# A gated delta rule: two products of the scan made as one, the last transposed update left out, and the inverse's first triangle made one round earlier

## The chip, the cores and the metric

One core of a Trainium2 chip runs the whole kernel in one launch. The metric is the device time in microseconds (us) of that launch; of several runs, the median.

## What is computed

Two transformer blocks over 1024 tokens of width 1024, all in float32. The change touches one branch of the first block, the gated delta rule: 4 heads, keys and values of width 128, chunks of 64 tokens.

```python
kk = jnp.einsum('bhnid,bhnjd->bhnij', k, k)
m = jnp.where(strict, beta[..., :, None] * kk * decay, 0.0)
rhs = jnp.concatenate([beta[..., None] * v, beta[..., None] * k * jnp.exp(gc)[..., None]], axis=-1)
sol = lax.linalg.triangular_solve(eye + m, rhs, left_side=True, lower=True, unit_diagonal=True)
u, w = sol[..., :dv], sol[..., dv:]
...
def step(state, inp):
    qk_c, qd_c, kd_c, u_c, w_c, ge_c = inp
    v_new = u_c - jnp.einsum('bhck,bhkv->bhcv', w_c, state)
    o = (jnp.einsum('bhck,bhkv->bhcv', qd_c, state)
         + jnp.einsum('bhij,bhjv->bhiv', qk_c, v_new))
    state = state * ge_c[..., None, None] + jnp.einsum('bhck,bhcv->bhkv', kd_c, v_new)
    return state, o
```

So a chunk multiplies two matrices with the same state: w (64 by 128) and the decayed q (64 by 128).

## The kernel before, in words

The kernel is a row of phases with a barrier of all engines between them; SBUF and PSUM tiles are placed anew in each. The phase "delta" holds the change. Five stages share it, and each stage is a generator per engine that emits a piece of its instructions and yields. `run_stages` goes through one written-out list of stage numbers, the plan, and lets each engine's generators emit in that order. An engine runs its own instructions strictly in the order emitted; engines meet only through semaphores (`ev.wait` before, `ev.done` behind an instruction).

`delta_plan` (L1508) makes the plan from rounds: 3 opening rounds and then 10 periods of 14 rounds (s = 0 to 13). In each round come in this order

- DeltaFront (L949): in period t it prepares the tile of 128 tokens (two chunks) number t: turns q, k and v, norms, the decay matrix, `mt` (the masked product m, transposed; round 10), `qk_t` (round 11).
- DeltaBack (L1190): one period later it inverts eye + m for the tile, by 5 levels of block doubling. Round 0: the first triangle on VectorE, `bt0` and `upper0` (L1227, L1229: 128 by 512 each), four transposes of it on TensorE (L1268) and ScalarE's copy to `lower`. Then for each level an odd round with `bx` (L1277) and an even round with the two updates (L1284 for `lower`, L1285 for its transpose `upper`) and VectorE's two subtractions (L1233, L1234). Round 11: u (L1291); round 12: w (L1296), whose copy to SBUF is L1238.
- DeltaScan (L1301): one period later again it runs the recurrence over the tile's two chunks. In rounds 1 and 7 (`FIRST`) w by state (L1377) and q by state (L1382); in rounds 3 and 9 (`SECOND`) the growth of the state (L1390) and qk by v_new (L1394).
- TokenProjection (L1400): a projection of all tokens, 10 groups of 256 columns; one step of it is 12 matmuls in fp32r (L1500 to L1502); 162 steps are spread evenly over the rounds, mostly one each, sometimes two. Every fourth step ends with a copy on VectorE (L1486) and every fourth with one on ScalarE (L1476); two steps in sixteen split the next weights (ScalarE L1453, VectorE L1458).

GpSimd makes, among others, `vb` (L1114, round 12), `wr` (L1118, round 13) and the masked `bt` of each level (L1248; levels 1 and 2 in rounds 0 and 1).

A float32 product of one head is two instructions for TensorE, so the four heads show as x8; a transpose is one, so x4; an fp32r product is one.

The order of the rounds is what the change works on:

```python
        if t < TT:
            plan.append(0)
        if 1 <= t <= TT:
            plan.append(1)
        if t >= 2:
            plan.append(2)
        ...
        plan += [3] * (want - given)
```

Of the kernel before, what the change touches and what calls it, by code (L numbers as in the profile page):

```python
# [808 lines left out]
class Delta:  # L809
# [4 lines left out]
    def __init__(self, ph, nc, early, qkv, out, c):  # L814
        self.nc, self.early, self.c, self.qkv, self.out = nc, early, c, qkv, out
        H = self.H
        self.ba = ph.sb("ba", [P, TT, 2 * H])
        self.a_row, self.dt_row, self.mask, self.exp_a = early.a_row, early.dt_row, early.mask, ph.sb("exp_a", [P, H])
        self.x, self.clip, self.expx, self.softplus, self.g, self.rest = (
            ph.sb(n, [P, TT, H]) for n in ("x", "clip", "expx", "softplus", "g", "rest"))  # L820
        self.by_tile = ph.sb("by_tile", [P, TT, 4, H])
        self.beta, self.g_sum, self.exp_gc, self.exp_rest = (self.by_tile[:, :, i, :] for i in range(4))
        self.chunk_decay = ph.sb("chunk_decay", [P, 2, TT, H])
        self.xt, self.tok, self.t_sb = ph.sb("xt", [P, 3 * H, P]), ph.sb("tok", [P, 3, H, P]), ph.sb("t_sb", [P, 3, H, P])
        self.norm = ph.sb("norm", [P, 3, 2 * H])
        self.half = ph.sb("half", [P, 2 * H])
        (self.kn, self.qn, self.kb, self.vb, self.wr, self.qd, self.gb, self.decay, self.mt, self.upper, self.lower, self.bx,
         self.u, self.w_t, self.faded) = (
            ph.sb(n, [P, H, P]) for n in ("kn", "qn", "kb", "vb", "wr", "qd", "gb", "decay", "mt", "upper", "lower", "bx",
                                          "u", "w_t", "faded"))  # L830
        two = lambda n: [ph.sb(f"{n}{i}", [P, H, P]) for i in range(2)]
        self.bt, self.q_t, self.qk_t, self.k_end, self.state, self.v_new, self.o_sb = (
            two(n) for n in ("bt", "q_t", "qk_t", "k_end", "state", "v_new", "o"))
        self.front = [ph.ps(f"front{i}", [P, H, P]) for i in range(2)]
        self.back = [ph.ps(f"back{i}", [P, H, P]) for i in range(2)]
        self.ws, self.o = ph.ps("ws", [P, H, P]), ph.ps("o_acc", [P, H, P])
        self.xt_in, self.stored = ph.sem("xt_in"), ph.sem2("stored")
        self.pre = Events(ph, "pre", ["turned", "kept", "half", "exp_a", "beta", "x", "clip",
                                      "expx", "log", "softplus", "g", "sums", "gc", "rest", "exps"])
        self.ev = Events(ph, "tile", [  # L840
            "q_turned", "k_turned", "v_turned", "gc_rows", "kn_turned", "kb_turned", "qn_turned", "qd_turned", "kk", "qk_dot",
            "gb", "tok_q", "tok_k", "tok_v", "squares", "decay", "t_k", "t_kb", "t_q", "q_kept",
            "sums", "gap", "clamp", "kn", "kb", "qn", "masked", "mt", "qk",
            "means", "inverse", "k_end", "qd", "vb", "wr",
            "bt0", "upper0", "lower0_t", "lower0", "bt", "bx", "bx_kept", "update", "lower", "upper", "u_dot", "u", "w_dot", "w",
            "ws", "v_new", "faded", "grow", "state", "o_done", "o_out"])
# [4 lines left out]
    def over_heads(self, a):  # L851
        return a.unsqueeze(1).to_broadcast([P, self.H, P])


# [94 lines left out]
class DeltaFront:  # L949
# [18 lines left out]
    def scalar(self, act):  # L968
# [17 lines left out]
        for j in range(TT):  # L986
            for s in range(d.STEPS):
# [31 lines left out]
                elif s == 9:  # L1019
                    ev.wait(act, "qd_turned", j + 1)  # L1020
                    ev.wait(act, "o_done", 2 * (j - 1))
                    ev.done(nc.scalar.activation(d.q_t[j % 2][:], d.front[1][:], ACT.Copy), "q_kept")
                yield

    def vector(self, dve):
        d, ev, pre, nc, H = self.d, self.d.ev, self.d.pre, self.d.nc, self.d.H
        sums = lambda b: d.o[:, b, 0:TT * H].rearrange("p (m h) -> p m h", h=H)
        pre.wait(dve, "turned", 1)
        pre.done(nc.vector.tensor_copy(d.ba[:], d.ws[:, 0, 0:2 * TT * H].rearrange("p (m n) -> p m n", n=2 * H)), "kept")
        pre.wait(dve, "kept", 1)  # L1030
# [17 lines left out]
        for j in range(TT):  # L1048
            for s in range(d.STEPS):
# [28 lines left out]
                elif s == 11:  # L1078
                    ev.wait(dve, "qk_dot", j + 1)
                    ev.wait(dve, "o_done", 2 * (j - 1))  # L1080
                    ev.done(nc.vector.tensor_tensor(d.qk_t[j % 2][:], d.front[1][:], d.decay[:], ALU.mult), "qk")
                yield

# [37 lines left out]
    def tensor(self, pe):  # L1121
# [3 lines left out]
        for m in range(TT):  # L1125
            last = nc.tensor.transpose(d.ws[:, 0, m * 2 * H:(m + 1) * 2 * H], d.early.ba_t[:, m * P:(m + 1) * P],
                                       ident[0:2 * H, 0:2 * H])
# [62 lines left out]
class DeltaBack:  # L1190
# [28 lines left out]
    def vector(self, dve):  # L1219
        d, ev, nc, L = self.d, self.d.ev, self.d.nc, self.d.LEVELS  # L1220
        for j in range(TT):
            for s in range(d.STEPS):
                if s == 0:
                    ev.wait(dve, "mt", j + 1)
                    ev.wait(dve, "w_dot", j)
                    ev.wait(dve, "u_dot", j)
                    ev.done(nc.vector.tensor_tensor(d.upper[:], d.mt[:], d.over_heads(d.mask[:, 0, :]), ALU.mult), "bt0")  # L1227
                    ev.wait(dve, "bt0", j + 1)
                    ev.done(nc.vector.tensor_tensor(d.upper[:], d.over_heads(d.c["ident"][:]), d.upper[:], ALU.subtract), "upper0")  # L1229
# [28 lines left out]
    def tensor(self, pe):  # L1258
        d, ev, nc, H, L = self.d, self.d.ev, self.d.nc, self.d.H, self.d.LEVELS
        for j in range(TT):  # L1260
            for s in range(d.STEPS):
# [17 lines left out]
                elif s <= 2 * L and s % 2 == 0:  # L1279
# [21 lines left out]
class DeltaScan:  # L1301
# [8 lines left out]
    def chunk(self, i):  # L1310
        return i // 2, slice((i % 2) * CHUNK, (i % 2 + 1) * CHUNK), i % 2

    def sync(self, sp):
        d, ev = self.d, self.d.ev
        for j in range(TT):
            for s in range(d.STEPS):
                if s in (5, 11):
                    i = 2 * j + (s == 11)
                    _, rows, p = self.chunk(i)
                    ev.wait(sp, "o_out", i + 1)  # L1320
                    sp.dma_start(d.out[i * CHUNK:(i + 1) * CHUNK, :].rearrange("t (h d) -> t h d", d=P), d.o_sb[p][rows]
                                 ).then_inc(d.stored[p], 16)
# [7 lines left out]
    def scalar(self, act):  # L1330
        d, ev, nc = self.d, self.d.ev, self.d.nc
        for j in range(TT):
            for s in range(d.STEPS):
                if s in self.SECOND:
# [3 lines left out]
                    if i >= 2:  # L1338
                        act.wait_ge(d.stored[p], 16 * (i // 2))
                    ev.done(nc.scalar.activation(d.o_sb[p][rows], d.o[rows], ACT.Copy), "o_out")  # L1340
                yield

    def vector(self, dve):
        d, ev, nc, H = self.d, self.d.ev, self.d.nc, self.d.H
        ev.done(nc.vector.memset(d.state[0][:], 0.0), "state")
        for j in range(TT):
            for s in range(d.STEPS):
                if s in self.FIRST:
# [4 lines left out]
                    ev.wait(dve, "o_done", i - 1)  # L1353
                    ev.done(nc.vector.tensor_tensor(d.v_new[p][rows], d.u[rows], d.ws[rows], ALU.subtract), "v_new")
                    ev.wait(dve, "state", i + 1)
                    ev.done(nc.vector.tensor_tensor(d.faded[:], d.state[p][:], d.per_head(d.chunk_decay[:, i % 2, m, :]), ALU.mult),
                            "faded")
                elif s in self.SECOND:
# [4 lines left out]
                    ev.wait(dve, "o_done", i)  # L1363
                    ev.done(nc.vector.tensor_tensor(d.state[1 - p][:], d.faded[:], d.ws[:], ALU.add), "state")
                yield

    def tensor(self, pe):
        d, ev, nc, H = self.d, self.d.ev, self.d.nc, self.d.H
        for j in range(TT):
            for s in range(d.STEPS):  # L1370
                if s in self.FIRST:
# [3 lines left out]
                    ev.wait(pe, "w", j + 1)  # L1375
                    for h in range(H):
                        last = nc.tensor.matmul(d.ws[rows, h, :], d.w_t[:, h, rows], d.state[p][:, h, :], start=True, stop=True)  # L1377
                    ev.done(last, "ws")
                    ev.wait(pe, "q_kept", j + 1)
                    ev.wait(pe, "o_out", i)  # L1380
                    for h in range(H):
                        nc.tensor.matmul(d.o[rows, h, :], d.q_t[j % 2][:, h, rows], d.state[p][:, h, :], start=(h == 0), stop=False,  # L1382
                                         skip_group_check=True)
                elif s in self.SECOND:
# [4 lines left out]
                    for h in range(H):  # L1389
                        last = nc.tensor.matmul(d.ws[:, h, :], d.k_end[j % 2][rows, h, :], d.v_new[p][rows, h, :], start=True, stop=True)  # L1390
# [3841 lines left out]
```

## Time and profile before

| | us |
|---|---|
| median of 3 runs | 2673.11 |
| lowest, highest | 2672.35, 2676.2 |
| the profiled execution's own time | 2669.34 |
| its span, first to last instruction | 2667.6 |
| TensorE busy in the span | 2545.4 (95%) |
| VectorE, ScalarE, GpSimd busy | 1455.6 (55%), 998.5 (37%), 350.5 (13%) |
| mean granted TensorE clock | 0.983 of full speed |

The engines are PE (TensorE; PEld its weight loads), DVE (VectorE), ACT (ScalarE), POOL (GpSimd). Matmuls are pipelined: the duration shown of one is longer than the distance to the next, so the distance from start to start is what one costs. "Idle before" is time in which the engine had nothing under way, and the arrow names what ended it. A clock of 1.00 is 2.4 GHz, 0.50 is 1.2 GHz.

### The profile page before, as it was taken

To read this page: it belongs to the slowest core of one execution; us is meant where nothing else is said; L and a number is where in the kernel's file an instruction comes from. 1 tells how busy PE (TensorE), PEld (TensorE's weight loads), DVE (VectorE), ACT (ScalarE), POOL (GpSimd) and SP (SyncE) were. 2 spreads that over 40 slices of the span, in tenths; PEclk is the share of its full clock that TensorE was granted. 3 is DMA by queue.
4 is the path that set the end of the run, shared out by engine and by line. 5 is a ranking of instruction groups with operands and counts; after the bars stand their busy time and mean duration, and the time that the engine had idled before them with its cause. 6 is when DMAs were issued, how large, how long until landed. Compare 5 with 4: busy or idle time off the path is not lost. (4 is left out here: it accounts for less than half of the span.)

```text
span 2667.6 us, 37142 instructions
## 1 busy us (share of the span) xinstructions
PE 2545.4 (95%) x14438; PEld 2189.2 (82%) x14438; DVE 1455.6 (55%) x2148; ACT 998.5 (37%) x1721; POOL 350.5 (13%) x450
## 2 busy tenths in 40 slices
PE   7999999999899997999997998999899999999999
PEld 6879999998688886888896786878788888888887
DVE  6544443442467763635225867644888777733452
ACT  4232222221455662223114776643433333322331
POOL 1002222220233310001002322101000000000000
PEclk9999999999999998999998998999999999999999
DMA  4321221112433214343234211154322222254532
GB/s 140 117 101 53 65 67 50 55 40 54 133 106 95 81 59 174 134 154 114 85 102 150 56 40 53 50 174 141 68 95 76 82 79 95 92 190 169 186 110 83
DMA packets 215847, 264.77 MB, mean 99 GB/s; under 512 B 46932, under 2 KB 147924, under 8 KB 215672
## 3 DMA queue, kind: packets, MB, share of 16 engines
q1 hardware_dynamic: 215672, 262.38, 30.4%
q8 instruction: 116, 1.90, 0.3%
q14 instruction: 59, 0.48, 0.1%
HBM read 185.11 MB, written 77.22 MB: 98 GB/s over the span
## 5 line engine op out<-in xcount | busy, mean ns | idle before, releaser
L4623 DVE TENSOR_TENSOR ffn_feed_lo<-ffn_feed_raw,ffn_feed_hi 128x1536 fp32r<-128x1536 f32 x44 | 77.4, 1759 | 143.7 <-ACT ffn_feed_hi L4614 143.7
L4323 PE MATMUL ffn_up_acc<-mixed_hi,ffn_ring_hi 128*128 128x512 f32 x348 | 135.6, 390 | 1.7 <-DVE ffn_gain_row L4243 1.3
L4323 PE MATMUL ffn_up_acc<-mixed_hi,ffn_ring_lo 128*128 128x512 f32 x348 | 135.4, 389 | 0.0
L4323 PE MATMUL ffn_up_acc<-mixed_lo,ffn_ring_hi 128*128 128x512 f32 x348 | 135.4, 389 | 0.0
L4614 ACT ACTIVATE ffn_feed_hi<-ffn_feed_raw 128x1536 fp32r<-128x1536 f32 x44 | 65.4, 1487 | 168.5 <-PE ffn_up_acc L4693 162.8
L445 DVE TENSOR_TENSOR_SCAN stick_keep<-stick_keep,stick_zero 128x127 f32<-128x127 f32 (+7 forms) x64 | 92.8, 1451 | 56.6 <-ACT stick_keep L393 55.9
L652 PE MATMUL stick_g_acc<-xn_hi,stick_g_hi 128*128 128x512 f32 x256 | 109.0, 426 | 7.2 <-DVE stick_g_lo L630 6.1
L4693 PE MATMUL ffn_up_acc<-ffn_feed_hi 128*128 128x512 f32 x352 | 108.5, 389 | 0.0
L4693 PE MATMUL ffn_up_acc<-ffn_feed_hi,ffn_feed_lo 128*128 128x512 f32 x352 | 108.3, 389 | 0.0
L4693 PE MATMUL ffn_up_acc<-ffn_feed_lo,ffn_feed_hi 128*128 128x512 f32 x352 | 108.3, 389 | 0.0
L653 PE MATMUL stick_g_acc<-xn_lo,stick_g_hi 128*128 128x512 f32 x256 | 103.1, 403 | 0.0
L654 PE MATMUL stick_g_acc<-xn_hi,stick_g_lo 128*128 128x512 f32 x256 | 102.7, 401 | 0.0
L1500 PE MATMUL delta_acc<-delta_w_hi,xn_hi 128*128 128x256 f32 x320 | 96.1, 300 | 0.0
L1500 PE MATMUL delta_acc<-early_w_hi,xn_hi 128*128 128x256 f32 x320 | 95.9, 300 | 0.0
L4119 ACT ACTIVATE ffn_ring_hi<-ffn_xn 128x512 fp32r<-128x512 f32 x88 | 54.9, 629 | 107.0 <-PE ffn_up_acc L4323 66.6
L1502 PE MATMUL delta_acc<-delta_w_hi,xn_lo 128*128 128x256 f32 x320 | 90.9, 284 | 0.0
L1501 PE MATMUL delta_acc<-delta_w_lo,xn_hi 128*128 128x256 f32 x320 | 90.8, 284 | 0.0
L1502 PE MATMUL delta_acc<-early_w_hi,xn_lo 128*128 128x256 f32 x320 | 90.4, 282 | 0.0
L1501 PE MATMUL delta_acc<-early_w_lo,xn_hi 128*128 128x256 f32 x320 | 90.4, 282 | 0.0
L4717 POOL TENSOR_SCALAR ffn_tail_mean<-ffn_tail_total 128x1 f32<-128x1 f32 x8 | 3.8, 476 | 654.6 <-ACT ffn_tail_gate L4732 654.3
L2262 PE MATMUL trunk_turn<-trunk_mla_v,trunk_mla_weight_t 128*128 128x64 f32 x576 | 73.3, 273 | 13.1 <-DVE trunk_mla_o L2180 11.7
L2241 PE MATMUL trunk_z<-trunk_mla_k_t,trunk_mla_q_t 96*128 96x512 f32 (+3 forms) x192 | 76.9, 511 | 7.2 <-DVE trunk_diff_neg_top L2488 6.8
(504 smaller groups left out, 7464.9 us busy)
## 6 DMA issues: line engine op xcount, KB each, us to landing
ffn_feed_raw<-in_w_down SPq DMA_DIRECT2D x44, 512.0 KB, 4.1
ffn_ring_raw<-in_w_gate SPq DMA_DIRECT2D x11, 1024.0 KB, 5.2
ffn_ring_raw<-in_w_up SPq DMA_DIRECT2D x11, 1024.0 KB, 5.2
scratch_act_t<-ffn_silu SPq DMA_DIRECT2D x22, 512.0 KB, 3.0
ffn_feed_raw<-scratch_act_t SPq DMA_DIRECT2D x44, 256.0 KB, 2.9
early_w_raw<-in_w_in SPq DMA_DIRECT2D x20, 512.0 KB, 5.0
scratch_projected<-delta_out SPq DMA_DIRECT2D x80, 128.0 KB, 1.7
early_g_raw<-in_w_in SPq DMA_DIRECT2D x16, 512.0 KB, 5.1
```

Of the source, the lines that this page charges most:

```text
L445: nc.vector.tensor_tensor_scan(back, back, self.zero[:].to_broadcast([P, n - 1]), 1.0, ALU.mult, ALU.add).then_inc(self.scanned, 1)
L652: nc.tensor.matmul(self.acc[:], w_hi, self.hi[:, k, cols], start=(k == 0), stop=False, skip_group_check=True)
L653: nc.tensor.matmul(self.acc[:], w_hi, self.lo[:, k, cols], start=False, stop=False, skip_group_check=True)
L654: last = nc.tensor.matmul(self.acc[:], w_lo, self.hi[:, k, cols], start=False, stop=(k == self.kt - 1), skip_group_check=True)
L1500: nc.tensor.matmul(acc, self.hi[:, k, tok], w_hi, start=(k == 0), stop=False, skip_group_check=True)
L1501: nc.tensor.matmul(acc, self.hi[:, k, tok], w_lo, start=False, stop=False, skip_group_check=True)
L1502: last = nc.tensor.matmul(acc, self.lo[:, k, tok], w_hi, start=False, stop=(k == self.kt - 1), skip_group_check=True)
L2241: last = nc.tensor.matmul(self.z.tile(("mla", u))[:, c0:c0 + w], self.q_t[t % 2][:, h, :], self.k_t[:, h, c0:c0 + w], start=True, stop=True)
L2262: last = nc.tensor.matmul(self.o[:, h, :], self.weight_t[u % 2][:, kb * P:(kb + 1) * P], self.v_sb[:, kb, t // TT * H + h, :], start=(h == ...
L4323: last = nc.tensor.matmul(self.bank(u, product), weight[:, k], x[:, k], start=(k == 0 and first and product not in (2, 4)), stop=(k == 3 a ...
L4623: self.nc.vector.tensor_tensor(self.lo[s][:], self.raw[s][:], self.hi[s][:].bitcast(F32), ALU.subtract).then_inc(self.lo_done[s], 1)
L4693: last = nc.tensor.matmul(t.pairs[j][:, half, :], part, weight[:, HALF + half * HALF:HALF + (half + 1) * HALF], start=begins, stop=ends, s ...
```

## The change

1. One product in place of two (rounds 1 and 7 of the scan). The transposes of w and q lie side by side in one tile `w_q`, two buffers, 64 columns of w beside 64 of q for each head and chunk. One product by the state gives both in the bank `d.o`: in the even chunk rows 0 to 63 are w by state and 64 to 127 q by state, in the odd chunk the other way round. The output of a chunk then stands in the other half of the rows (`o_rows`), and qk by v_new goes from the chunk's rows into that other half. The one product waits for all four events: state, w, q_kept and o_out. The copies of w (VectorE) and q (ScalarE) write in pieces of 64. The growth of the state has a bank of its own (`grown`).
2. In level 5 the update of `lower`, its transposed partner being the one that is used on, is left out: 4 products (L1284) and one subtraction (L1233) a tile.
3. `bt0` and `upper0` go from round 0 of DeltaBack to round 13 of DeltaFront, that is in VectorE's order ahead of the token projection's pieces of round 13, in place of behind them.

The diff, with plain renamings (`ws` to `grown` in the opening, `self.o_rows(i)` in the store) left out:

```diff
--- before.py
+++ after.py
@@ class Delta @@
-        self.bt, self.q_t, self.qk_t, self.k_end, self.state, self.v_new, self.o_sb = (
-            two(n) for n in ("bt", "q_t", "qk_t", "k_end", "state", "v_new", "o"))
+        self.bt, self.qk_t, self.k_end, self.state, self.v_new, self.o_sb = (
+            two(n) for n in ("bt", "qk_t", "k_end", "state", "v_new", "o"))
+        self.w_q = [ph.sb(f"w_q{i}", [P, 2 * 9 * CHUNK]) for i in range(2)]
...
-        self.ws, self.o = ph.ps("ws", [P, H, P]), ph.ps("o_acc", [P, H, P])
+        self.grown, self.o = ph.ps("grown", [P, H, P]), ph.ps("o_acc", [P, H, P])
...
+    def by_chunk(self, a):
+        return a.rearrange("p h (s t) -> p s h t", t=CHUNK)
+
+    def w_parts(self, j):
+        return self.w_q[j % 2][:].rearrange("p (s g t) -> p s g t", g=9, t=CHUNK)[:, :, 0:8:2, :]
+
+    def q_parts(self, j):
+        return self.w_q[j % 2][:, CHUNK:15 * CHUNK].rearrange("p (s g t) -> p s g t", g=7, t=CHUNK)[:, :, 0:7:2, :]
+
+    def w_and_q(self, j, part, h):
+        at = (part * self.H + h) * P
+        return self.w_q[j % 2][:, at:at + P]
@@ DeltaFront.scalar @@
-                    ev.done(nc.scalar.activation(d.q_t[j % 2][:], d.front[1][:], ACT.Copy), "q_kept")
+                    ev.done(nc.scalar.activation(d.q_parts(j), d.by_chunk(d.front[1][:]), ACT.Copy), "q_kept")
@@ DeltaFront.vector @@
+                elif s == 13:
+                    ev.wait(dve, "mt", j + 1)
+                    ev.wait(dve, "w_dot", j)
+                    ev.wait(dve, "u_dot", j)
+                    ev.done(nc.vector.tensor_tensor(d.upper[:], d.mt[:], d.over_heads(d.mask[:, 0, :]), ALU.mult), "bt0")
+                    ev.wait(dve, "bt0", j + 1)
+                    ev.done(nc.vector.tensor_tensor(d.upper[:], d.over_heads(d.c["ident"][:]), d.upper[:], ALU.subtract), "upper0")
@@ DeltaBack.scalar @@
-                    ev.wait(act, "lower", L * j)
+                    ev.wait(act, "lower", (L - 1) * j)
@@ DeltaBack.vector @@
-                if s == 0:
...
-                elif s <= 2 * L and s % 2 == 0:
+                if 0 < s <= 2 * L and s % 2 == 0:
                     n = L * j + s // 2
                     ev.wait(dve, "update", n)
-                    ev.done(nc.vector.tensor_tensor(d.lower[:], d.lower[:], d.back[1][:], ALU.subtract), "lower")
+                    if s < 2 * L:
+                        ev.done(nc.vector.tensor_tensor(d.lower[:], d.lower[:], d.back[1][:], ALU.subtract), "lower")
                     ev.done(nc.vector.tensor_tensor(d.upper[:], d.upper[:], d.back[0][:], ALU.subtract), "upper")
                 elif s == 12:
                     ev.wait(dve, "w_dot", j + 1)
-                    ev.wait(dve, "ws", 2 * j)
-                    ev.done(nc.vector.tensor_copy(d.w_t[:], d.back[0][:]), "w")
+                    ev.wait(dve, "ws", 2 * (j - 1))
+                    ev.done(nc.vector.tensor_copy(d.w_parts(j), d.by_chunk(d.back[0][:])), "w")
@@ DeltaBack.tensor @@
                     for h in range(H):
-                        nc.tensor.matmul(d.back[1][:, h, :], d.upper[:, h, :], d.bx[:, h, :], start=True, stop=True)
+                        if level < L:
+                            nc.tensor.matmul(d.back[1][:, h, :], d.upper[:, h, :], d.bx[:, h, :], start=True, stop=True)
                         last = nc.tensor.matmul(d.back[0][:, h, :], d.bx[:, h, :], d.upper[:, h, :], start=True, stop=True)
@@ DeltaScan @@
+    def o_rows(self, i):
+        return slice((1 - i % 2) * CHUNK, (2 - i % 2) * CHUNK)
...
-                    ev.done(nc.scalar.activation(d.o_sb[p][rows], d.o[rows], ACT.Copy), "o_out")
+                    o_rows = self.o_rows(i)
+                    ev.done(nc.scalar.activation(d.o_sb[p][o_rows], d.o[o_rows], ACT.Copy), "o_out")
...
-                    ev.done(nc.vector.tensor_tensor(d.v_new[p][rows], d.u[rows], d.ws[rows], ALU.subtract), "v_new")
+                    ev.done(nc.vector.tensor_tensor(d.v_new[p][rows], d.u[rows], d.o[rows], ALU.subtract), "v_new")
...
-                    ev.done(nc.vector.tensor_tensor(d.state[1 - p][:], d.faded[:], d.ws[:], ALU.add), "state")
+                    ev.done(nc.vector.tensor_tensor(d.state[1 - p][:], d.faded[:], d.grown[:], ALU.add), "state")
@@ DeltaScan.tensor @@
                     ev.wait(pe, "state", i + 1)
                     ev.wait(pe, "w", j + 1)
-                    for h in range(H):
-                        last = nc.tensor.matmul(d.ws[rows, h, :], d.w_t[:, h, rows], d.state[p][:, h, :], start=True, stop=True)
-                    ev.done(last, "ws")
                     ev.wait(pe, "q_kept", j + 1)
                     ev.wait(pe, "o_out", i)
                     for h in range(H):
-                        nc.tensor.matmul(d.o[rows, h, :], d.q_t[j % 2][:, h, rows], d.state[p][:, h, :], start=(h == 0), stop=False,
-                                         skip_group_check=True)
+                        last = nc.tensor.matmul(d.o[:, h, :], d.w_and_q(j, p, h), d.state[p][:, h, :], start=(h == 0),
+                                                stop=False, skip_group_check=True)
+                    ev.done(last, "ws")
...
-                        last = nc.tensor.matmul(d.o[rows, h, :], d.qk_t[j % 2][rows, h, rows], d.v_new[p][rows, h, :], start=False,
+                        last = nc.tensor.matmul(d.o[self.o_rows(i), h, :], d.qk_t[j % 2][rows, h, rows], d.v_new[p][rows, h, :], start=False,
                                                 stop=(h == H - 1), skip_group_check=True)
```

## Rows read from the trace of the kernel before

**Rows 1.** Two stretches: their us, busy us of each engine, PEclk, DMA share, GB/s.
```profile
173.70:661.15 487.45, 478.26 (x3984) 462.93 (x3984) 194.95 (x289) 130.13 (x222) 107.43 (x97) 1.00 0.21 61
310.00:318.00 8.00, 5.36 (x35) 5.12 (x34) 4.03 (x4) 1.58 (x3) 2.79 (x2) 0.79 0.06 18
```

**Rows 2.** TensorE's waits from 173 to 665 us.
```profile
PE delta_back L1268 <- DVE delta_upper L1229: 8.5, 6, 2.6
```

**Rows 3.** Timeline of TensorE around a round 7 (start, us, engine, line).
```profile
396.12 0.60 PE L1140 MATMUL delta_front<-ident,delta_kb 128*128 128x128 f32 x4
396.56 1.06 PE L1277 MATMUL delta_back<-delta_lower,delta_bt 128*128 128x128 f32 x8
397.54 1.09 PE L1377 MATMUL delta_ws<-delta_state,delta_w_t 128*64 128x128 f32 x8
398.47 1.04 PE L1382 MATMUL delta_o_acc<-delta_state,delta_q_t 128*64 128x128 f32 x8
399.43 0.39 PE L1500 MATMUL delta_acc<-early_w_hi,xn_hi 128*128 128x256 f32 x1
...
401.41 0.39 PE L1284 MATMUL delta_back<-delta_bx,delta_upper 128*128 128x128 f32 x2
```

**Rows 4.** Timeline of TensorE, two products of full shape between others.
```profile
303.86 1.05 PE L1185 MATMUL delta_front<-delta_t_sb 128*128 128x128 f32 x8
304.75 1.06 PE L1291 MATMUL delta_back<-delta_vb,delta_upper 128*128 128x128 f32 x8
305.57 0.37 PE L1500 MATMUL delta_acc<-delta_w_hi,xn_hi 128*128 128x256 f32 x1
```

**Rows 5.** Timeline of TensorE, the updates of level 5 (round 10).
```profile
412.01 0.39 PE L1284 MATMUL delta_back<-delta_bx,delta_upper 128*128 128x128 f32 x2
...
413.58 0.39 PE L1285 MATMUL delta_back<-delta_upper,delta_bx 128*128 128x128 f32 x2
413.72 0.37 PE L1500 MATMUL delta_acc<-delta_w_hi,xn_hi 128*128 128x256 f32 x1
```

**Rows 6.** Timeline of three engines from period 2 to period 3.
```profile
309.62 0.42 DVE L1486 COPY delta_out<-delta_acc 128x256 f32<-128x256 f32 x1 [0.75 <-PE delta_acc L1502]
309.97 1.70 DVE L1458 TENSOR_TENSOR early_w_lo<-early_w_raw,early_w_hi 128x1024 fp32r<-128x1024 f32 x1
313.37 0.69 DVE L1229 TENSOR_TENSOR delta_upper<-ident,delta_upper 128x512 f32<-128x512 f32 x1
...
309.29 3.49 POOL L1248 TENSOR_TENSOR delta_bt<-delta_mt,early_mask 128x512 f32<-128x512 f32 x2
...
310.87 0.60 PE L1140 MATMUL delta_front<-ident,delta_xt 128*128 128x128 f32 x4
314.11 1.11 PE L1268 MATMUL delta_back<-ident,delta_upper 128*128 128x128 f32 x4 [2.64 <-DVE delta_upper L1229]
```

**Rows 7.** Timeline from period 6 to period 7.
```profile
528.66 0.69 DVE L1238 COPY delta_w_t<-delta_back 128x512 f32<-128x512 f32 x1 [2.54 <-PE delta_back L1296]
529.27 1.09 DVE L1227 TENSOR_TENSOR delta_upper<-delta_mt,early_mask 128x512 f32<-128x512 f32 x1
530.39 1.67 DVE L1229 TENSOR_TENSOR delta_upper<-ident,delta_upper 128x512 f32<-128x512 f32 x1
...
532.12 0.66 PE L1268 MATMUL delta_back<-ident,delta_upper 128*128 128x128 f32 x4 [0.17 <-DVE delta_upper L1229]
```

**Rows 8.** Timeline from period 4 to period 5.
```profile
419.56 0.69 DVE L1238 COPY delta_w_t<-delta_back 128x512 f32<-128x512 f32 x1 [2.54 <-PE delta_back L1296]
...
422.25 0.60 PE L1140 MATMUL delta_front<-ident,delta_xt 128*128 128x128 f32 x4
424.52 0.66 PE L1268 MATMUL delta_back<-ident,delta_upper 128*128 128x128 f32 x4 [1.67 <-DVE delta_upper L1229]
```

**Rows 9.** Timeline of ScalarE in rounds 3 and 7 of one period.
```profile
385.24 0.59 ACT L1340 ACTIVATE delta_o<-delta_o_acc 64x512 f32<-64x512 f32 x1 [1.50 <-PE delta_o_acc L1394]
...
397.65 0.60 ACT L1212 ACTIVATE delta_bx<-delta_back 128x512 f32<-128x512 f32 x1 [0.30 <-PE delta_back L1277]
```

More of the change, by code:

```diff
@@ L827, in __init__ @@
         (self.kn, self.qn, self.kb, self.vb, self.wr, self.qd, self.gb, self.decay, self.mt, self.upper, self.lower, self.bx,
-         self.u, self.w_t, self.faded) = (
+         self.u, self.faded) = (
             ph.sb(n, [P, H, P]) for n in ("kn", "qn", "kb", "vb", "wr", "qd", "gb", "decay", "mt", "upper", "lower", "bx",
-                                          "u", "w_t", "faded"))
+                                          "u", "faded"))
         two = lambda n: [ph.sb(f"{n}{i}", [P, H, P]) for i in range(2)]
-        self.bt, self.q_t, self.qk_t, self.k_end, self.state, self.v_new, self.o_sb = (
-            two(n) for n in ("bt", "q_t", "qk_t", "k_end", "state", "v_new", "o"))
+        self.bt, self.qk_t, self.k_end, self.state, self.v_new, self.o_sb = (
+            two(n) for n in ("bt", "qk_t", "k_end", "state", "v_new", "o"))
+        self.w_q = [ph.sb(f"w_q{i}", [P, 2 * 9 * CHUNK]) for i in range(2)]
         self.front = [ph.ps(f"front{i}", [P, H, P]) for i in range(2)]
         self.back = [ph.ps(f"back{i}", [P, H, P]) for i in range(2)]
-        self.ws, self.o = ph.ps("ws", [P, H, P]), ph.ps("o_acc", [P, H, P])
+        self.grown, self.o = ph.ps("grown", [P, H, P]), ph.ps("o_acc", [P, H, P])
         self.xt_in, self.stored = ph.sem("xt_in"), ph.sem2("stored")
@@ L1028, in vector @@
         pre.wait(dve, "turned", 1)
-        pre.done(nc.vector.tensor_copy(d.ba[:], d.ws[:, 0, 0:2 * TT * H].rearrange("p (m n) -> p m n", n=2 * H)), "kept")
+        pre.done(nc.vector.tensor_copy(d.ba[:], d.grown[:, 0, 0:2 * TT * H].rearrange("p (m n) -> p m n", n=2 * H)), "kept")
         pre.wait(dve, "kept", 1)
@@ L1125, in tensor @@
         for m in range(TT):
-            last = nc.tensor.transpose(d.ws[:, 0, m * 2 * H:(m + 1) * 2 * H], d.early.ba_t[:, m * P:(m + 1) * P],
+            last = nc.tensor.transpose(d.grown[:, 0, m * 2 * H:(m + 1) * 2 * H], d.early.ba_t[:, m * P:(m + 1) * P],
                                        ident[0:2 * H, 0:2 * H])
@@ L1222, in vector @@
             for s in range(d.STEPS):
-                if s == 0:
[L1224 to L1229, printed above, removed]
-                elif s <= 2 * L and s % 2 == 0:
+                if 0 < s <= 2 * L and s % 2 == 0:
                     n = L * j + s // 2
                     ev.wait(dve, "update", n)
-                    ev.done(nc.vector.tensor_tensor(d.lower[:], d.lower[:], d.back[1][:], ALU.subtract), "lower")
+                    if s < 2 * L:
+                        ev.done(nc.vector.tensor_tensor(d.lower[:], d.lower[:], d.back[1][:], ALU.subtract), "lower")
                     ev.done(nc.vector.tensor_tensor(d.upper[:], d.upper[:], d.back[0][:], ALU.subtract), "upper")
@@ L1320, in sync @@
                     ev.wait(sp, "o_out", i + 1)
-                    sp.dma_start(d.out[i * CHUNK:(i + 1) * CHUNK, :].rearrange("t (h d) -> t h d", d=P), d.o_sb[p][rows]
+                    sp.dma_start(d.out[i * CHUNK:(i + 1) * CHUNK, :].rearrange("t (h d) -> t h d", d=P), d.o_sb[p][self.o_rows(i)]
                                  ).then_inc(d.stored[p], 16)
@@ L1389, in tensor @@
                     for h in range(H):
-                        last = nc.tensor.matmul(d.ws[:, h, :], d.k_end[j % 2][rows, h, :], d.v_new[p][rows, h, :], start=True, stop=True)
+                        last = nc.tensor.matmul(d.grown[:, h, :], d.k_end[j % 2][rows, h, :], d.v_new[p][rows, h, :], start=True, stop=True)
                     ev.done(last, "grow")
```

## The prediction

> **What bounds the kernel now.** First the busy time of the delta phase's stretch. TensorE is busy for 478.3 of 487.5 us, VectorE for 195, ScalarE for 130, GpSimd for 107, at the full clock, 2.4 GHz [rows 1]. So this phase lasts as long as TensorE's list of instructions, and the projection's last product ends it. The next phase begins behind a barrier; nothing in it looks at an absolute time. What leaves TensorE's list here should leave the kernel. Then TensorE's waits: one line of the code has nearly all of them, the four transposes of the first triangle, L1268, 8.5 us in 6 of 8 tiles, the longest 2.6 us, all on VectorE's `upper0` [rows 2]. Last the timeline, from start to start, because the durations shown overlap.
>
> The sum is made against the profiled execution, 2669.34 us (span 2667.6). The median of the runs, 2673.11 us, is 3.8 us above it; I take the saving from the median.
>
> **Term A, one product in place of two.** In round 7 the scan's w product starts 0.98 us behind the bx product, q's 0.93 us later, and the projection 0.96 us behind that: 2.87 us for eight instructions of full shape and sixteen of 64 columns [rows 3]. In the changed kernel eight of full shape stand behind eight of full shape. The rows show such a pair: 0.89 us to the second, then 0.82 us to the projection, 1.71 us [rows 4]. That saves 1.16 us a chunk, 16 chunks: **18.6 us**. It is more than the 0.93 us of one group, since the step into and out of the 64 column shape costs some 0.1 us on either side. Bounds: if the one product with its four waits pays for both these steps still, one group of 0.93 us is saved, 14.9 us; if each of the two added waits cost 0.1 us on top, 12 us; above, 20 us. I take 18.6, since the rows at full shape are the same instruction form. Here a rule speaks against the change. The rows show sixteen instructions with 64 columns at 0.116 us each and those with 128 at 0.111, so half the columns do not halve the distance. The Trainium skill, "TensorE: Matmul & The Clock Gate", section "LDWEIGHTS (loading the stationary operand)", says a load takes time in proportion to its columns, whatever the rows: 53 ns for 64 and 107 ns for 128, as an estimate from its formula. Were the loads what paces this list, two narrow products would cost what one wide one does and term A would be nothing; this case's trace disagrees for the narrow ones.
>
> Product qk by v_new goes from the rows of the chunk to the other half of the output rows. No row shows this position. I take its cost as unchanged, and as a bound 0.1 us each way a chunk, the size of the shape steps above: 1.6 us up or down. The copies of w and q write pieces of 64 floats; by the nearest row, VectorE's whole copy of 0.69 us [rows 7], between no change and twice that. ScalarE's lies beside idle time. VectorE's stands ahead of `bt0`, so it counts only where term C still has a wait, at most 0.69 us in three places, 2 us. I take nothing.
>
> **Term B, level 5.** The sixteen instructions of both updates take 1.71 us, from 412.01 to 413.72 [rows 5]; eight take 0.82 us to the projection [rows 4]. That is 0.89 us in each of 8 tiles: **7.1 us**. VectorE loses a subtraction a tile, an operation of the same form as those of 0.69 us [rows 6], which stands on no path. It makes `upper` ready earlier, for u in round 11. Bounds 6.4 and 7.4.
>
> **Term C, the first triangle.** VectorE's order, not its load, makes L1268 late. From period 2 to 3 the w copy has long ended, but a projection copy at 309.62 and a split at 309.97, 1.70 us long, stand ahead of `bt0`; `upper0` ends at 314.06 and the transposes start at 314.11. TensorE was free for them at 311.31, that is 0.44 us behind the start of the q transposes at 310.87 [rows 3, 6]. The delay is 2.80 us, where the profile calls 2.64 of it idle. So the waits cost the 8.5 us of [rows 2] and 0.16 us six times, 9.5 us. From period 4 to 5 it was a copy of round 13 that stood ahead [rows 8].
>
> Now `bt0` comes ahead of the projection's pieces of round 13, but still behind those of round 12. How long the two operations then take is shown from 6 to 7, where nothing stood between: `bt0` starts 0.61 us behind the start of the w copy and `upper0` ends 2.79 us later. They take 2.79 in place of 1.38 us since GpSimd runs `wr` and two `bt` then [rows 7]. By boundary:
>
> - 2 to 3: the copy of round 12 stays ahead, the split doesn't. 309.97 + 2.79 = 312.76, against 311.31: a delay of 1.5 us in place of 2.8.
> - 4 to 5: 419.56 + 0.61 + 2.79 = 422.96, against 422.69: 0.3 in place of 1.83 [rows 8].
> - 6 to 7: unchanged, 0.33 (0.17 idle) [rows 7].
> - The other three (4.05 us idle together, 4.5 with their shares): two have two projection steps between w and the transposes and only their VectorE work of round 13 in the way, so nothing is left; one is like 2 to 3 with one more projection step, 0.1 us left.
>
> Left are 2.2 us, so **7.3 us** is saved. What is late next is the same `upper0` behind a copy of round 12 beside GpSimd. The longest stall also let the clock fall: 0.79 over the 8 us from 310 [rows 1], so 3.4 us of them at 1.2 GHz, with work in all but the first part; about **1.3 us** comes back, as a stall of 1.67 us [rows 8] left none. Added wait: `bt0` now holds VectorE in round 13 for w_dot, which the w copy ahead of it has already waited for, so nothing behind it waits longer; the projection's copy of round 13 ends up to 2.8 us later and its bank is wanted two steps of the projection on. Bounds of C with the clock: 3 us (GpSimd's share falls worse, as beside the split) and 10.8 us (all). The Trainium skill, "SBUF — State Buffer", section "Who interferes with whom", calls the pair of ports an exclusive lock held for a whole instruction, the other engine blocked. By it each triangle operation could wait out a GpSimd `bt`, and the two would take some 3.5 us: 0.7 us more at four boundaries. The trace has 2.79 us.
>
> What shrinks is cover. ScalarE's bx copy starts at 397.65 and ends at 398.25, and the update that needs it starts at 401.41 [rows 3, 9]. There are 3.1 us between; without 1.16 us of scan product 2 are left.
>
> **Sum:** 18.6 + 7.1 + 7.3 + 1.3 = 34.3 us, 1.3%. 2673.1 - 34.3 = 2638.8, near 2639 us.
>
> **Rivals.**
> 1. The stall stays: VectorE's round 12 pieces, two inputs of each triangle operation and GpSimd's three instructions bunch, as they now start together. For it: the 1.70 us operation beside `bt` of 3.49 us [rows 6]. Against: the clean case of 2.79 us [rows 7]. A and B alone: 25.7 us, 2647 us.
> 2. The loads pace the wide product, or its four waits and output rows eat term A. B, C and the clock alone: 15.7 us, 2657 us. Against: the distances in [rows 3, 4].
> 3. Slower: the bank `d.o` now takes w by state too, so v_new, and with it the state, waits for ScalarE's output copy (o_out) of the chunk before. This copy is in ScalarE's queue behind the projection's. It decides once a chunk's product waits more than 34.3 / 16 = 2.1 us for it; at 3 us each the kernel is 13.7 us slower, 2687 us. Against: the copy of round 3 ends at 385.83, the product of round 7 starts at 397.54, 11.7 us later [rows 3, 9].
> 4. The clock, or another stage's luck, gives or takes a few us: between executions the runs spread over 3.9 us. With a further fall avoided or the bounds above met at the good end, 2632 us.
> 5. The products are made and dropped, but TensorE's time doesn't matter: no change, 2673 us. Against: 98% busy, and no transfer or other engine near it [rows 1].
>
> **How the numbers follow.** Forecast 0.69, rival 1 0.15, rival 2 0.05, rival 3 0.03, rival 4 0.05, rival 5 0.03. The terms' bounds give savings from 24 to 38 us; with the spread of the runs the range is 2631 to 2651 us, which takes in rivals 1 and 4 and leaves out 2, 3 and 5 and tails. A measurement of this kernel tells about 0.2%, 5.3 us, from no change. Faster by more than that: forecast, rivals 1, 2 and 4, 0.94; within it rival 5, 0.03; slower rival 3, 0.03.
>
> **What would show it.** In rounds 1 and 7 one group x8 of form 128*128 in the place of two of 128*64, with 0.9 us before and 0.8 behind its start; if 1.0 and more, A was too large. L1284's counterpart x256 and round 10's updates 0.8 us long. L1268 with about 1.5 us of waits in two to four tiles, the longest 1.3 to 1.7, no clock below 1.00 between 300 and 330 us. The last projection product near 627 us in place of 661. A wait of TensorE on the output copy would make rival 3 right. Should the phase be 34 us shorter and the kernel not, the prediction's first step is wrong.

## The result, and the profile after

| | before | changed |
|---|---|---|
| median of 4 runs | 2672.73 us | 2638.36 us |
| lowest to highest | 2667.91 to 2676.2 | 2634.24 to 2640.87 |
| span of the profiled execution | 2667.6 | 2639.1 |
| TensorE busy in the span | 2545.4 | 2523.0 |
| first to last projection product of the delta phase | 174.25 to 661.01 | 173.71 to 625.54 |

The ratio is 0.988, 95% interval 0.9868 to 0.9892: faster by 34 us, or 1.2%. The forecast was 2639 us. The delta phase is 451.83 us long in place of 486.76, 34.9 us less.

Now the stretches of TensorE that the prediction priced, in the changed kernel. First the timeline around a round 7, the counterpart of [rows 3]:

```profile
281.32 1.06 PE L1292 MATMUL delta_back<-delta_lower,delta_bt 128*128 128x128 f32 x8
282.21 1.06 PE L1399 MATMUL delta_o_acc<-delta_state,delta_w_q 128*128 128x128 f32 x8
283.03 0.36 PE L1518 MATMUL delta_acc<-early_w_hi,xn_hi 128*128 128x256 f32 x1
```

From the start of bx (L1292) to the start of the one product it is 0.89 us, and from there to the projection 0.82: 1.71 us where 2.87 stood. Next round 10, the counterpart of [rows 5]:

```profile
295.58 1.06 PE L1301 MATMUL delta_back<-delta_upper,delta_bx 128*128 128x128 f32 x8
296.40 0.37 PE L1518 MATMUL delta_acc<-delta_w_hi,xn_hi 128*128 128x256 f32 x1
```

One group of eight is left, 0.82 us ahead of the projection. Then TensorE's waits from 165 to 620 us, for [rows 2]:

```profile
PE delta_back L1283 <- DVE delta_upper L1102: 1.7, 3, 1.4
PE delta_grown L1147 <- PEq L44: 1.6, 1, 1.6
```

The transposes wait 1.7 us in place of 8.5. Nearly all of it is at one boundary, from period 2 to 3. Here are the same three engines as in [rows 6]:

```profile
303.68 0.42 DVE L1504 COPY delta_out<-delta_acc 128x256 f32<-128x256 f32 x1 [0.75 <-PE delta_acc L1520]
304.02 1.17 DVE L1100 TENSOR_TENSOR delta_upper<-delta_mt,early_mask 128x512 f32<-128x512 f32 x1
305.22 1.64 DVE L1102 TENSOR_TENSOR delta_upper<-ident,delta_upper 128x512 f32<-128x512 f32 x1
306.78 1.21 DVE L1476 TENSOR_TENSOR early_w_lo<-early_w_raw,early_w_hi 128x1024 fp32r<-128x1024 f32 x1
...
303.35 2.96 POOL L1263 TENSOR_TENSOR delta_bt<-delta_mt,early_mask 128x512 f32<-128x512 f32 x2
...
304.92 0.60 PE L1161 MATMUL delta_front<-ident,delta_xt 128*128 128x128 f32 x4
306.91 0.66 PE L1283 MATMUL delta_back<-ident,delta_upper 128*128 128x128 f32 x4 [1.39 <-DVE delta_upper L1102]
```

The projection's copy still stands ahead of the two triangle operations (L1100, L1102), the split of weights (L1476) now behind them. The two last 2.84 us, from 304.02 to 306.86, beside GpSimd's two `bt`. The transposes start 1.99 us behind the start of the q transposes (304.92); less the 0.44 us that these take, the delay is 1.55 us. Over the seven boundaries with q transposes ahead the delays are 0, 0.14, 1.55, 0, 0.34, 0 and 0.34 us, 2.37 in all. Clock of this phase, and of the 10 us that hold this stall:

```profile
173.70:625.80 452.10, 449.68 (x3786) 439.58 (x3784) 194.07 (x281) 128.88 (x222) 108.96 (x96) 1.00 0.23 66
300.00:310.00 10.00, 8.61 (x74) 8.37 (x74) 4.97 (x5) 4.06 (x7) 5.00 (x4) 1.00 0.04 15
```

**Where 6 us of the profiled pair went.** The spans differ by 28.5 us, the phase by 34.9, the medians by 34.4. The first and last starts of some lines, before (first four) and changed (last four), place the difference:

```profile
L652 PE MATMUL stick_g_acc<-xn_hi,stick_g_hi x256: 388/398/792, 667.4 to 1020.4; 128*128 128x512 f32 x128
L2262 PE MATMUL trunk_turn<-trunk_mla_v,trunk_mla_weight_t x576: 219/275/421, 1445.9 to 1753.7; 128*128 128x64 f32 x192
L3801 PE MATMUL ffn_turn<-ident,ffn_mla x32: 270/272/273, 1775.9 to 1832.6; 128*128 128x128 f32 x32
L4693 PE MATMUL ffn_up_acc<-ffn_feed_hi x352: 389/389/477, 2327.2 to 2566.4; 128*128 128x512 f32 x176
```
```profile
L652 PE MATMUL stick_g_acc<-xn_hi,stick_g_hi x256: 388/398/795, 631.9 to 985.5; 128*128 128x512 f32 x128
L2280 PE MATMUL trunk_turn<-trunk_mla_v,trunk_mla_weight_t x576: 219/275/422, 1410.4 to 1721.5; 128*128 128x64 f32 x192
L3819 PE MATMUL ffn_turn<-ident,ffn_mla x32: 270/272/273, 1744.0 to 1803.9; 128*128 128x128 f32 x32
L4711 PE MATMUL ffn_up_acc<-ffn_feed_hi x352: 389/389/477, 2298.8 to 2537.9; 128*128 128x512 f32 x176
```

The first product of L652, in the next phase, and the first of L2262, in the second block's attention (1445.9 to 1410.4), both start 35.5 us earlier; the last of L2262 is 32.2 us earlier, the last of the next turn (L3801) 28.7, and it stays so to the end. The granted clock of these two stretches, before (first two) and changed (last two):

```profile
1445.90:1753.70 307.80, 278.15 (x1856) 232.07 (x1855) 215.95 (x589) 210.96 (x490) 75.51 (x115) 0.96 0.17 48
1775.90:1832.60 56.70, 54.78 (x270) 45.43 (x269) 35.66 (x57) 24.40 (x33) 8.33 (x18) 1.00 0.69 234
```
```profile
1410.40:1721.50 311.10, 282.12 (x1855) 235.30 (x1854) 217.00 (x592) 211.43 (x490) 76.75 (x115) 0.94 0.17 48
1744.00:1803.90 59.90, 56.42 (x270) 46.66 (x269) 35.71 (x56) 24.02 (x33) 10.68 (x18) 0.97 0.66 220
```

Both became longer, by 3.3 and 3.2 us, and both have a lower clock in the changed kernel's profile, 0.94 against 0.96 and 0.97 against 1.00. The change touches no instruction of theirs. The same shows between executions of one kernel: the runs of the changed kernel with a mean clock of 0.981 took 2640.9 and 2640.2 us, those with 0.985 took 2634.2 and 2636.5. So the lost 6 us go with the clock of later stages. What makes the clock differ there was not tried. The parts below are read by the length of the delta phase, where instructions that an edit leaves alone are spaced alike in all profiles at the full clock, with the run times beside them.

### The profile page after: what moved, and what is told of

Read it like the earlier page. It is cut to its first block and busy times, and to the rows that moved or that the text cites. A ratio compares the mean times of both kernels' runs of the same rounds, so it can differ in the third digit from the quotient of the medians.

```text
span 2639.1 us, 36749 instructions
## 1 busy us (share of the span) xinstructions
PE 2523.0 (96%) x14246; PEld 2171.1 (82%) x14246; DVE 1455.1 (55%) x2140; ACT 997.3 (38%) x1721; POOL 354.6 (13%) x450
## 5 line engine op out<-in xcount | busy, mean ns | idle before, releaser
L652 PE MATMUL stick_g_acc<-xn_hi,stick_g_hi 128*128 128x512 f32 x256 | 109.1, 426 | 7.2 <-DVE stick_g_lo L630 6.1
L2280 PEld LDWEIGHTS trunk_turn<-trunk_mla_v,trunk_mla_weight_t 128*128 128x128 f32 x576 | 71.1, 196 | 16.3 <-ACT trunk_mla_weight_t L2112 10.6
```

Source lines behind the costliest of these rows:

```text
L652: nc.tensor.matmul(self.acc[:], w_hi, self.hi[:, k, cols], start=(k == 0), stop=False, skip_group_check=True)
L2280: last = nc.tensor.matmul(self.o[:, h, :], self.weight_t[u % 2][:, kb * P:(kb + 1) * P], self.v_sb[:, kb, t // TT * H + h, :], start=(h == ...
```

## The experiments

All lengths are from the start of the first to the start of the last projection product, in one profiled execution each.

| kernel | phase, us | against | median, us | ratio to before, 95% |
|---|---|---|---|---|
| before | 486.76 | | 2672.0 | |
| changed | 451.83 | -34.93 before | 2638.36 | 0.988 (0.9868 to 0.9892) |
| joined_alone | 466.38 | -20.38 before | 2651.76 | 0.9933 (0.9921 to 0.9945) |
| level5_alone | 481.14 | -5.62 before | 2666.06 | 0.9983 (0.9972 to 0.9994) |
| triangle_alone | 478.17 | -8.59 before | 2662.42 | 0.9971 (0.9959 to 0.9982) |
| two_narrow | 464.79 | +12.96 changed | 2649.67 | 0.9924 (0.9911 to 0.9937) |
| narrow_in_turn | 457.02 | +5.19 changed | 2644.1 | 0.9895 (0.9878 to 0.9912) |
| bt_later | 449.48 | -2.35 changed | 2636.64 | 0.9872 (0.9856 to 0.9888) |
| bx_other_bank | 447.86 | -3.97 changed | 2634.66 | 0.9871 (0.9851 to 0.9891) |
| bt_and_bx | 446.94 | -4.89 changed | 2633.72 | 0.986 (0.9844 to 0.9876) |

(The kernel before ran at 2672.7 us beside the changed one, at 2672.0 beside the first four experiments and at 2671.3 beside the last four; the ratios are to these.)

**The three parts alone.** joined_alone has only the part of the diff on `w_q`, `grown` and the product; level5_alone only `if level < L` and its two companions; triangle_alone only the move of `bt0` and `upper0`.

> Part 1 of the change alone on the kernel before. Theory (TensorE's list paces the phase, 1.16 us a chunk leave it): 18.6 us faster; the stretch bx product to projection in rounds 1 and 7 is 1.71 us in place of 2.87; the transposes L1268's counterpart keep 8 to 9 us of waits. Rival (the shorter list only makes TensorE wait more elsewhere): under 12 us faster, with new waits of TensorE of 6 us or more in this phase.

> Part 2 alone on the kernel before. Theory: 0.89 us in each of 8 tiles, 7.1 us faster, and nothing else moves. Rival (cover of other work is lost): 0 to 4 us, with TensorE waiting in rounds 10 to 12.

> Part 3 alone on the kernel before. Theory: the delay of the transposes falls from 9.5 to 2.2 us, with the clock some 8.6 us faster. Rival (GpSimd beside the two operations takes it back): 3 us or less, with delays of 1 us or more at four boundaries.

The phase gets 20.4, 5.6 and 8.6 us shorter, 34.6 together against 34.9 for the whole change: the parts add up, and none takes another's place. To compare each with its forecast the clock has to be taken out. In the trace of before it fell once in this phase, behind the stall of 2.64 us [rows 1, 6]. joined_alone keeps this stall. Its transposes from period 2 to 3, the bx product behind them, and the clock of the 20 us around:

```profile
311.27 0.66 PE L1282 MATMUL delta_back<-ident,delta_upper 128*128 128x128 f32 x4 [2.64 <-DVE delta_upper L1243]
313.63 1.06 PE L1291 MATMUL delta_back<-delta_lower,delta_bt 128*128 128x128 f32 x8
```
```profile
300.00:320.00 20.00, 17.36 (x150) 17.12 (x150) 9.06 (x11) 6.76 (x11) 5.53 (x4) 1.00 0.12 34
```

The same wait, and no fall. The same two instructions in before, where the transposes start at 314.11 [rows 6], and then in level5_alone, where the clock fell behind the stall too:

```profile
317.80 1.06 PE L1277 MATMUL delta_back<-delta_lower,delta_bt 128*128 128x128 f32 x8
```
```profile
314.07 0.81 PE L1269 MATMUL delta_back<-ident,delta_upper 128*128 128x128 f32 x4 [2.64 <-DVE delta_upper L1229]
317.98 1.06 PE L1278 MATMUL delta_back<-delta_lower,delta_bt 128*128 128x128 f32 x8
```

From the transposes to bx, with the same instructions between, it is 2.36 us at the full clock, 3.69 in before and 3.91 in level5_alone. So the fall cost before 1.33 us and level5_alone 1.55. In level5_alone the clock was low in the first 10 us of the phase as well:

```profile
170.00:180.00 10.00, 8.40 (x52) 6.78 (x50) 0.60 (x3) 4.41 (x8) 0.11 (x1) 0.83 0.54 163
300.00:320.00 20.00, 17.36 (x137) 17.00 (x136) 7.16 (x8) 5.22 (x9) 5.53 (x4) 0.91 0.11 33
```

Its first transposes of a triangle start 40.25 us behind the first projection product, in before 38.75: 1.50 us lost. At one clock the three parts are then these:

- joined_alone: 20.4 - 1.3 = 19.1 us, 18.6 expected. The priced steps (into and out of the one product) give 18.75 of them.
- level5_alone: 5.6 + 1.5 + 0.2 = 7.3 us, 7.1 expected (0.2 because its fall cost 1.55 us and the one of before 1.33).
- triangle_alone, whose clock is 1.00 throughout: 8.6 - 1.3 = 7.3 us, 7.3 expected. The delays of the transposes themselves fall from 9.5 to 2.4 us, by 7.1.

The rivals of all three fall: TensorE's waits in joined_alone and level5_alone are the 8.5 us of before and no new ones, and in triangle_alone 1.7 us. By run times level5_alone is at the edge of what can be told from no change, with 0.9983.

**Is it the merging, or the instructions' width?** two_narrow:

```diff
-                    for h in range(H):
-                        last = nc.tensor.matmul(d.o[:, h, :], d.w_and_q(j, p, h), d.state[p][:, h, :], start=(h == 0),
-                                                stop=False, skip_group_check=True)
+                    for part in (rows, self.o_rows(i)):
+                        for h in range(H):
+                            last = nc.tensor.matmul(d.o[part, h, :], d.w_and_q(j, p, h)[:, part], d.state[p][:, h, :],
+                                                    start=(h == 0), stop=False, skip_group_check=True)
```

> The changed kernel with its one wide product a head made again as two of 64 columns, from the same tile into the same bank; all else as changed. Theory (a product costs 0.11 us an instruction whatever its columns, and 0.1 us for the step into and out of the 64 column shape): 16 to 19 us slower than the changed kernel, 1.9 us a chunk in place of 0.81. Rival (loads pace the products, in proportion to their columns): the same time as the changed kernel within 3 us.

A miss in the size: 13.0 us of phase, 11.3 us of median, below the 16 expected but far from the rival's 3. TensorE around a round 7:

```profile
282.14 1.06 PE L1292 MATMUL delta_back<-delta_lower,delta_bt 128*128 128x128 f32 x8
283.13 1.58 PE L1400 MATMUL delta_o_acc<-delta_state,delta_w_q 128*64 128x128 f32 x16
284.64 0.39 PE L1519 MATMUL delta_acc<-early_w_hi,xn_hi 128*128 128x256 f32 x1
```

The step into the narrow shape is 0.99 us in place of 0.89 with one wide product, as it is 0.98 in [rows 3]. But the sixteen take 1.51 us in place of 1.89: in before both groups went to the same half of the columns, here the second goes to the other. The single starts are 283.13, .29, .40, .51, .62, .62, .73, .78, .83, .89, .94, 284.00, .11, .22, .33 and .44. The trace doesn't name the half of an instruction, but the sixteen can be read as two rows of eight, one from 283.13 and one from 283.62, each with a first step of 0.16 us and then 0.11: the second half starts 0.49 us behind the first and runs beside it until 283.94. The six close starts in the middle are 0.055 us apart on the mean, and the next expectation takes this for the distance from one half to the other. narrow_in_turn swaps the two loops (`for h` outside, `for part` inside), so that the halves take turns:

> As two_narrow, the changed kernel's one wide product a head made again as two of 64 columns, but the two halves of the columns take turns head by head, in place of four heads of one half and then four of the other. Theory (products into the same half of the columns follow at 0.11 us, into the other half at 0.055, as the few instructions at the change of half showed): the sixteen take 0.9 to 1.1 us in place of 1.51, so some 7 us faster than two_narrow and 3 to 6 us slower than the changed kernel. Rival (the closeness at the change of half was one merely of that moment): 1.5 us or more, the time of two_narrow.

```profile
281.94 1.06 PE L1292 MATMUL delta_back<-delta_lower,delta_bt 128*128 128x128 f32 x8
282.92 1.09 PE L1400 MATMUL delta_o_acc<-delta_state,delta_w_q 128*64 128x128 f32 x16
283.95 0.39 PE L1519 MATMUL delta_acc<-early_w_hi,xn_hi 128*128 128x256 f32 x1
```

1.03 us for the sixteen, and 5.2 us of phase against the changed kernel: the time is as expected. The spacing isn't. The sixteen are eight pairs: the two of a pair start 0.007 us apart, and the pairs follow at 0.16 us once and then at 0.11 (282.92, 283.08, .19, .30, .41, .52, .63, .74). So each half of the columns keeps the distance of 0.11 us by itself, and the two halves run side by side as far as the program's order lets them; 0.055 us is a mean and no distance of its own. With that the cost of narrow products is an effect of their order. In the same half of the columns sixteen cost 1.89 us [rows 3], one half after the other 1.51, in turn 1.03, and one product of full width 0.82.

**What is left of the stall.** bt_later makes GpSimd's `bt` wait for `upper0` in place of `mt`:

> The changed kernel with GpSimd's first two bt of a tile made to wait for upper0, so that they no longer run beside the two triangle operations. Theory (the two take 2.8 us in place of 1.4 because of GpSimd): bt0 and upper0 together 1.4 to 1.9 us, the transposes' delay over all tiles down from 2.4 to 0.8 us or less, the phase 1 to 2 us shorter, which the run times can hardly tell. Rival (the copy of round 12 ahead of them sets the delay, or the later bt makes bx wait): delay as before, or a new wait of TensorE for bt in round 1.

VectorE, GpSimd and TensorE from period 2 to 3:

```profile
303.17 0.68 DVE L1100 TENSOR_TENSOR delta_upper<-delta_mt,early_mask 128x512 f32<-128x512 f32 x1
303.88 0.69 DVE L1102 TENSOR_TENSOR delta_upper<-ident,delta_upper 128x512 f32<-128x512 f32 x1
...
304.66 3.44 POOL L1263 TENSOR_TENSOR delta_bt<-delta_mt,early_mask 128x512 f32<-128x512 f32 x2 [2.12 <-DVE delta_upper L1102]
...
304.07 0.60 PE L1161 MATMUL delta_front<-ident,delta_xt 128*128 128x128 f32 x4
304.63 0.66 PE L1283 MATMUL delta_back<-ident,delta_upper 128*128 128x128 f32 x4
```

The two operations take 1.40 us in place of 2.84, and the delay is 0.56 - 0.44 = 0.12 us in place of 1.55. In the five later tiles they take 1.8 us, since GpSimd's `wr` still runs beside `bt0`, which lasts 1.09 us there. Over the seven boundaries the delays sum to 0.1 us, and TensorE's waits on `upper0` are gone from the view. No wait for the later `bt` came in their place. The phase is 2.35 us shorter, a little above the 1 to 2 expected: it is the 2.2 us of delays and not more. It is shown that GpSimd's `bt` made the two operations long, and that this set what was left of the stall.

**The smaller wait in rounds 3 and 5.** In the changed kernel bx goes to `back[0]`, which VectorE empties last, with `upper`. bx_other_bank writes bx to `back[1]`, which VectorE reads first. The part of its edit on TensorE's waits (ScalarE's copy reads `back[1]` too, and in level 1 the wait for `u` moves to bx):

```diff
-                        ev.wait(pe, "upper", n - 1)
+                        ev.wait(pe, "lower", (L - 1) * j + level - 1)
...
-                        last = nc.tensor.matmul(d.back[0][:, h, :], d.bt[n % 2][:, h, :], d.lower[:, h, :], start=True, stop=True)
+                        last = nc.tensor.matmul(d.back[1][:, h, :], d.bt[n % 2][:, h, :], d.lower[:, h, :], start=True, stop=True)
...
+                    if level > 1:
+                        ev.wait(pe, "upper", n - 1)
```

> The changed kernel with bx written to the second bank of DeltaBack, which VectorE reads first, so that bx waits for lower alone and the update for upper. Theory (in rounds 3 and 5 bx stands 0.2 us late behind upper, 15 times): these steps fall from 1.12 to 0.89 and from 0.31 to 0.12 us, the phase 3 us shorter. Rival (the late step has another cause, or the update waits in its place): no change, or waits of 0.2 us in the even rounds.

The step from the decay rows to bx in round 3, in the changed kernel and then here:

```profile
316.16 1.05 PE L1180 MATMUL delta_front<-chunk_upto,delta_gb 128*128 128x128 f32 x8
317.28 1.13 PE L1292 MATMUL delta_back<-delta_lower,delta_bt 128*128 128x128 f32 x8
```
```profile
315.69 1.05 PE L1180 MATMUL delta_front<-chunk_upto,delta_gb 128*128 128x128 f32 x8
316.58 1.06 PE L1293 MATMUL delta_back<-delta_lower,delta_bt 128*128 128x128 f32 x8
```

1.12 us become 0.89, and the phase loses 4.0 us, where 3 were expected. The two late steps of a tile, 14 in all, give 2.9 of them: TensorE had been late by 0.2 us at each, in time that the profile counts as busy and that the view of waits doesn't list. The even rounds got no new wait. What follows bx got 0.07 us shorter as well, which was not expected and makes up the rest (the step to the growth of the state is 0.99 throughout, where it was 1.06 in 8 of 14 cases). Why it did is open.

> The changed kernel with bt_later and bx_other_bank both. Theory: the two are independent, 4 to 5 us shorter than the changed kernel in the phase, near 0.17%. Rival: one takes the other's place, 3 us or less.

Together 4.9 us. But the first 10 us of the phase had a clock of 0.83 in this profile, and its first transposes start 40.23 us behind the first projection product, where the changed kernel has 38.75. Without these 1.5 us it is 6.4, and the two edits alone give 2.35 + 3.97 = 6.3. So they are independent, as the theory says; that the phase came out inside the 4 to 5 us expected is luck, one gain larger than thought and a low clock against it. The ratio 0.986 (0.9844 to 0.9876) against the changed kernel's 0.988 (0.9868 to 0.9892) overlaps: this is the fastest version by its phase and its median, but run times can't tell it from the changed kernel.

## Why the prediction was right

At one clock the phase lost 19.1 us by the joined product, 7.3 by level 5 and 7.1 by the triangle's order, and 1.3 us of clock: 34.8 of the 34.9 measured, where 18.6, 7.1, 7.3 and 1.3 were forecast. The mechanism of each term held.

**The bound.** TensorE's list set the length of the phase, and what left it left the kernel, 34.9 us of phase and 34.4 us of median. The rival in which TensorE's time doesn't matter is out. That the median came within 1 us of the forecast is in part luck: the runs of the changed kernel spread over 6.6 us, and the profiled pair alone would have said 28.5.

**Term A, 18.6 us.** Right, per chunk to the hundredth: 1.71 us. Over the chunks the profile has 0.89 us before and 0.81 behind the product. joined_alone gives 19.1 us without the clock. The four waits on one product cost nothing that shows. The second rival (wide loads pace it) is out: the two narrow products of two_narrow take 1.51 us and the wide one 0.82, where by this rival both would take the same; in turn the narrow ones still take 1.03. What the prediction said beside it, 0.11 us whatever the columns, holds for narrow products in the same half of the columns only. One step of the sum of bounds is loose: the text names 12 us as the lowest value of A, but the savings "from 24 to 38 us" start from 14.9; with 12 they would start at 21.

**qk by v_new in the other half of the rows.** The bound of 1.6 us was not needed: 1.02 us from it to the projection in both kernels.

**Term B, 7.1 us.** Right: 0.89 us less in round 10, and 7.3 us in level5_alone at one clock.

**Term C, 7.3 us.** The delays left were forecast as 0.1, 1.5, 0.3 and 0.33 us and are 0.14, 1.55, 0.34 and 0.34. That came from reading the 2.79 us of [rows 7] as the price beside GpSimd, and bt_later shows that this was the cause. The rival in which the stall stays is out. The prediction gave some 3.5 us as the estimate by the exclusive lock of the Trainium skill, "SBUF — State Buffer", section "Who interferes with whom", without its working; the two took 2.84. The page says "for the whole instruction" of VectorE's 2-port modes; of an operation with two inputs in SBUF it says only that it contends with a GpSimd instruction that reads SBUF, and with that the trace agrees.

**The clock, 1.3 us.** The size was right, 1.33 us. Yet it is the weakest step, because joined_alone had the same stall without the fall. All that can be said is that two of three profiled executions with the stall had the fall there, and none of the seven without it. It is a matter of chance in an execution and belongs in the range, not in the sum.

**The slower rival** is out: no wait of TensorE on the output copy is in the list of waits.

**Cover.** As forecast, 2 us are left between ScalarE's bx copy and the update that needs it: in the changed kernel the copy of round 7 runs from 282.41 to 283.01 and the update starts at 284.98. The two waits of 0.2 us in rounds 3 and 5 were there before and were not named, because they stand in no view of waits; the change left them alone: 1.12 and 0.31 us from the step ahead of them in both kernels.

## What to carry to other kernels

Where one engine runs its list without a gap, price a change by the distance from start to start of the same instruction form next to the same neighbours; such distances, with the longest stall read beside them, gave the phase within 2% of its change. Compare profiles only after taking out what the clock cost, from the distance of two instructions that all of them have. Look at what stands ahead in the queue of the engine that ends a wait, and at what the third engine does beside it: at the worst boundary half of the triangle operations' time was GpSimd. If narrow products can't be joined into one wide, let them take turns between the halves of the columns.

## What the runs showed of the hardware that was not expected

- Products of 64 columns (float32, 128 columns moving) follow each other at 0.11 us in one half of TensorE's columns, and the other half keeps the same distance beside it: in narrow_in_turn the two of a pair start 0.007 us apart, sixteen take 1.03 us. The Trainium skill, "TensorEngine Tiling (Array Packing)", section "Tiling Modes", says that different tiles can load and multiply in parallel, and that a change of tiling mode drains the engine. The trace agrees with the first; it is in line with the second in that the step into the 64 column shape took 0.99 us where it takes 0.89 without.
- A stall of 2.64 us was followed by a fall of the clock to 1.2 GHz in two of three profiled executions that had it, at a cost of 1.33 and 1.55 us, and the phase began at a clock of 0.83 in two of ten, at 1.5 us.
- The two triangle operations of VectorE, both with two inputs in SBUF, took 0.69 us each alone and up to 1.77 us beside GpSimd's operations; GpSimd's `bt` lengthened too, from 1.3 to 1.74 us.
